# A fused attention layer on one core: another order for the first four projection units, and the first compression layer in pairs

## What is computed

```
h = rmsnorm(x, g_norm)
proj = einsum('bsd,de->bse', h, w_in)               # 2048 -> 7704 columns
... = split(proj)                                   # q, k, v, z of MoBA; q, 3 x (k, v), gates, z of NSA
y_moba = rmsnorm(o_moba * silu(m_z), g_out_moba)    # full causal attention here, since 256 tokens are one block
k_c = silu(flat(n_kc blocks + pe_ck) @ w_ck1) @ w_ck2   # 15 blocks of 32 tokens, 4096 -> 256 -> 128, per kv group
v_c = silu(flat(n_vc blocks + pe_cv) @ w_cv1) @ w_cv2
o_nsa = gates0 * compressed + gates1 * selected + gates2 * window
out = rmsnorm(x + concat(y_moba, rmsnorm(o_nsa * silu(n_z), g_out_nsa)) @ w_out, g_final)
```

## Time and profile before

| | us |
|---|---|
| time, median of 3 runs | 513.79 (513.75 to 514.21) |
| the profiled execution's own time | 515.05 |
| its span, first to last instruction | 513.2 |
| TensorE busy in the span | 502.2 (98%) |
| VectorE busy | 294.5 (57%) |
| ScalarE busy | 234.7 (46%) |
| GpSimd busy | 63.0 (12%) |
| mean granted TensorE clock | 0.997 |

### The profile page before, as it was taken

One profiled execution on the slowest core, in us unless ns is written; L12 is line 12 of the kernel. 1 busy time (PEld: TensorE's weight loads), 2 busy tenths in 40 slices (PEclk: granted clock), 3 DMA queues, 4 the chain that ended last, 5 costly groups with the idle time before them and its releaser, 6 DMA issues.

```text
span 513.2 us, 6503 instructions
## 1 busy us (share of the span) xinstructions
PE 502.2 (98%) x2600; PEld 415.8 (81%) x2600; DVE 294.5 (57%) x476; ACT 234.7 (46%) x323; POOL 63.0 (12%) x68
## 2 busy tenths in 40 slices
PE   7999999999999999999999999999999999999993
PEld 6878777777888888888888888888888888888882
DVE  3697434424475765955574675655366666645541
ACT  3585242434354453354345344545454562545421
POOL 3231000001010210100021030002131030011020
PEclk9999999999999999999999999999999999999998
DMA  8889469694526354344434435444985447275313
GB/s 284 294 256 358 165 247 318 243 331 134 197 90 191 137 164 137 112 163 140 152 119 163 128 119 175 156 162 141 370 307 167 163 165 245 83 245 205 123 44 120
DMA packets 53902, 96.45 MB, mean 188 GB/s; under 512 B 4240, under 2 KB 13040, under 8 KB 53488
## 3 DMA queue, kind: packets, MB, share of 16 engines
q1 hardware_dynamic: 50688, 95.43, 54.4%
q10 hardware_dynamic: 3184, 0.61, 0.7%
HBM read 93.93 MB, written 2.10 MB: 187 GB/s over the span
## 4 chain that ended last, share of the span: by engine, by line
PE 97%; DMA 1%; DVE 0%; ACT 0%; DVEq 0%; POOLq 0%; issue 0%; SPq 0%; POOL 0%
PE proj L433 27%; PE proj L435 27%; PE proj L434 27%; PE b_o L654 4%; PE b_t L419 2%; PE b_s L588 2%; PE b_s L531 2%; PE b_p L624 2%; PE b_t L678 1%; PE b_s L587 1%; DMA xo<-in_x_dram 1%; PE b_o L567 1%; PE b_o L419 0%; PE b_p L419 0%; PE b_s L419 0%; ACT raw_e L850 0%
## 5 line engine op out<-in xcount | busy, mean ns | idle before, releaser
L945 DVE TENSOR_TENSOR w_lo<-w_raw,w_hi 128x2048 fp32r<-128x2048 f32 x72 | 166.9, 2321 | 105.2 <-ACT w_hi L727 105.2
L433 PE MATMUL proj<-w_hi,xT_hi 128*128 128x512 f32 x536 | 216.6, 404 | 0.1
L435 PE MATMUL proj<-w_hi,xT_lo 128*128 128x512 f32 x536 | 209.3, 391 | 0.0
L434 PE MATMUL proj<-w_lo,xT_hi 128*128 128x512 f32 x536 | 208.7, 389 | 0.0
L727 ACT ACTIVATE w_hi<-w_raw 128x2048 fp32r<-128x2048 f32 x72 | 137.5, 1912 | 44.6 <-PE proj L435 35.4
L433 PEld LDWEIGHTS proj<-w_hi,xT_hi 128*128 128x128 f32 x536 | 100.7, 188 | 23.4 <-issue 3.6
L435 PEld LDWEIGHTS proj<-w_hi,xT_lo 128*128 128x128 f32 x536 | 100.6, 188 | 21.7
L434 PEld LDWEIGHTS proj<-w_lo,xT_hi 128*128 128x128 f32 x536 | 100.8, 188 | 19.9
L384 POOL TENSOR_TENSOR rope_a<-rope_a,rope_b 128x512 f32<-128x512 f32 (+1 forms) x16 | 24.2, 1534 | 237.9 <-DVE rope_b L1015 237.9
L779 ACT ACTIVATE Q<-b_t 128x512 f32<-128x512 f32 x18 | 10.8, 598 | 60.2 <-PE b_t L419 60.2
L791 ACT ACTIVATE pT<-b_p 128x384 f32<-128x384 f32 x24 | 11.7, 487 | 55.9 <-PE b_p L624 55.9
(11 more groups left out here) (187 smaller groups left out, 434.7 us busy)
## 6 DMA issues: line engine op xcount, KB each, us to landing
w_raw<-in_w_in_dram SPq DMA_DIRECT2D x57, 1024.0 KB, 5.2
w_raw<-in_w_out_dram SPq DMA_DIRECT2D x16, 1024.0 KB, 5.1
xo<-in_w_ck_dram SPq DMA_DIRECT2D x4, 1024.0 KB, 5.8
xo<-in_w_cv_dram SPq DMA_DIRECT2D x4, 1024.0 KB, 5.5
w_raw<-in_w_in_dram SPq DMA_DIRECT2D x12, 256.0 KB, 6.9
Q<-in_x_dram SPq DMA_DIRECT2D x1, 2048.0 KB, 10.9
out_dram<-Q SPq DMA_DIRECT2D x4, 512.0 KB, 3.1
xo<-in_x_dram SPq DMA_DIRECT2D x3, 512.0 KB, 8.0
```

Source lines behind the costliest of these rows:

```text
L433: nc.tensor.matmul(dst, a_hi, b_hi, start=first, stop=False)
L434: nc.tensor.matmul(dst, a_hi, b_lo, start=False, stop=False)
L435: return nc.tensor.matmul(dst, a_lo, b_hi, start=False, stop=last)
L945: nc.vector.tensor_tensor(wl, w_raw[:, u % RAW], wh.bitcast(F32), ALU.subtract).then_inc(lo_ready, 1)
```

## The change

Four things are edited.

1. The first four units on TensorE are written out in another order. A product now waits only for its own operands: hi·hi for `xT_hi` and `w_hi`, lo·hi (`LH`) for `xT_lo`, hi·lo (`HL`) for `w_lo`, which comes last in each unit. Rounds 2 and 3 come after 12 products of unit 0, rounds 4 and 5 after 8 of unit 1, rounds 6 and 7 after 8 of unit 2.
2. The start of TensorE: 6 identity products instead of 4, then the gain's transpose, then each of rounds 0 and 1 followed by one identity product and one identity transpose; the 15 identity products are gone.
3. The second half of the first quarter of x is issued by ScalarE's queue. ScalarE and VectorE do their pieces of units 0 to 3 in another order.
4. The pieces of the first compression layer are multiplied two by two, in slots 7, 10, 13 and 16, and have a load table of their own.

```diff
-NBUSY = 15
-X_ROUNDS_AT = {(0, 2): 2, (1, 2): 4, (1, 5): 6}
+ORDER_0 = [(HH, 0, 0), (HH, 0, 1), (LH, 0, 0), (LH, 0, 1), (HH, 1, 0), (HH, 1, 1), (HH, 0, 2), (LH, 0, 2), (HH, 0, 3), (LH, 0, 3),
+           (LH, 1, 0), (LH, 1, 1), (HH, 1, 2), (LH, 1, 2), (HH, 1, 3), (LH, 1, 3)] + [(HL, m, k) for k in range(UK) for m in range(MT)]
+X_ROUNDS_AT = {(0, 12): 2, (1, 8): 4, (2, 8): 6}
-CK_SLOT = [6, 7, 9, 10, 12, 13, 15, 16]
+CK_SLOT = [7, 7, 10, 10, 13, 13, 16, 16]
+CK_LOAD = [6, 7, 11, 12, 14, 15, 17, 18]
...
-                    for m in range(MT):
-                        sp.dma_start(xo[:, m, 0:CW], x[0, m * P:(m + 1) * P, 0:CW]).then_inc(x_in[4 * m], 16)
+                    sp.dma_start(xo[:, 0, 0:CW], x[0, 0:P, 0:CW]).then_inc(x_in[0], 16)
...
-                while ck_next < 8 and u >= CK_SLOT[ck_next] and u >= 6:
+                while ck_next < 8 and u >= CK_LOAD[ck_next]:
...
+                if kind == HH:
+                    if k == 0:
+                        pe.wait_ge(xhi_done, 2 * u + m + 1)
+                    if m == 0 and u < FIRST:
+                        pe.wait_ge(first_hi, u * UK + k + 1)
+                    if m == 0 and k == 0 and u == FIRST:
+                        pe.wait_ge(hi_ready, 1)
+                    return nc.tensor.matmul(dst, x_hi, w_hi_, start=u == 0 and k == 0, stop=False)
+                if kind == LH:
+                    if k == 0:
+                        pe.wait_ge((xlo_even, xlo_odd)[m], u + 1)
+                    return nc.tensor.matmul(dst, x_lo, w_hi_, start=False, stop=False)
+                if m == 0 and u < FIRST:
+                    pe.wait_ge(first_lo, u * UK + k + 1)
+                if m == 0 and k == 0 and u == FIRST:
+                    pe.wait_ge(lo_ready, 1)
+                return nc.tensor.matmul(dst, x_hi, w_lo_, start=False, stop=u == UPC - 1 and k == UK - 1)
...
             pe.wait_ge(ident_ok, 1)
-            keep_busy(4)
-            x_round_(0)
-            x_round_(1)
+            keep_busy(6)
             pe.wait_ge(grow_in, 16)
             nc.tensor.transpose(b_p[:, 0:KT], grows, ident[0:KT, 0:KT]).then_inc(crows_T, 1)
-            keep_busy(NBUSY)
+            x_round_(0)
+            keep_busy(1)
+            keep_busy_short(1)
+            x_round_(1)
+            keep_busy(1)
+            keep_busy_short(1)
...
             act.dma_start(grows, g_norm[0].rearrange("(k p) -> k p", p=P)).then_inc(grow_in, 16)
+            act.dma_start(xo[:, 1, 0:CW], x[0, P:2 * P, 0:CW]).then_inc(x_in[4], 16)
 
             x_hi(0)
-            first_hi_(0, [0])
+            first_hi_(0, [0, 1])
             x_hi(1)
-            first_hi_(0, [1, 2, 3])
+            first_hi_(0, [2, 3])
...
+                elif slot == 1:
                     x_g(6)
                     x_g(7)
-                    first_lo_(2, [1, 2, 3])
+                    lo(3)
                     x_lo(7)
```

More of the change, by code:

```diff
@@ L55 @@
 RAW, SPL = 3, 3
-NBUSY = 15
-X_ROUNDS_AT = {(0, 2): 2, (1, 2): 4, (1, 5): 6}
 FIRST = 3
+HH, LH, HL = 0, 1, 2
+ORDER_0 = [(HH, 0, 0), (HH, 0, 1), (LH, 0, 0), (LH, 0, 1), (HH, 1, 0), (HH, 1, 1), (HH, 0, 2), (LH, 0, 2), (HH, 0, 3), (LH, 0, 3),
+           (LH, 1, 0), (LH, 1, 1), (HH, 1, 2), (LH, 1, 2), (HH, 1, 3), (LH, 1, 3)] + [(HL, m, k) for k in range(UK) for m in range(MT)]
+ORDER_N = [(HH, m, k) for m in range(MT) for k in range(UK)] + [(LH, m, k) for m in range(MT) for k in range(UK)] + \
+          [(HL, m, k) for k in range(UK) for m in range(MT)]
+X_ROUNDS_AT = {(0, 12): 2, (1, 8): 4, (2, 8): 6}
 LAST = NSLOT - UPC
@@ L129, in heads_done @@
     return sum(ends_head(i) for i in range(j + 1))
-CK_SLOT = [6, 7, 9, 10, 12, 13, 15, 16]
-CK_AT = {s: c for c, s in enumerate(CK_SLOT)}
+CK_SLOT = [7, 7, 10, 10, 13, 13, 16, 16]
+CK_LOAD = [6, 7, 11, 12, 14, 15, 17, 18]
 CK_SUM_SLOT = [11, 17]
@@ L453, in bank_free, with first_product, first_unit @@
                     pe.wait_ge(dve_read, dve_reads(c - 2))
+            def first_product(u, kind, m, k):
+                dst, x_hi, x_lo, w_hi_, w_lo_ = operands(u, m, k)
+                if kind == HH:
[15 more added lines that the diff above has]
+                return nc.tensor.matmul(dst, x_hi, w_lo_, start=False, stop=u == UPC - 1 and k == UK - 1)
+            def first_unit(u):
+                for n, (kind, m, k) in enumerate(ORDER_0 if u == 0 else ORDER_N):
+                    if (u, n) in X_ROUNDS_AT:
+                        x_round_(X_ROUNDS_AT[u, n])
+                        x_round_(X_ROUNDS_AT[u, n] + 1)
+                    last = first_product(u, kind, m, k)
+                last.then_inc(unit_used, 1)
             def unit(u):
+                if u < UPC:
+                    return first_unit(u)
                 if u < NPROJ:
                     c, g = u // UPC, u % UPC
-                    if u < UPC:
-                        pe.wait_ge(xlo_even, u + 1)
-                        pe.wait_ge(xlo_odd, u + 1)
                 else:
@@ L466, in unit @@
                     bank_free(c)
[L467 to L478, removed]
+                pe.wait_ge(lo_ready, u - FIRST + 1)
+                for m in range(MT):
+                    for k in range(UK):
+                        last = three_products(*operands(u, m, k), g == 0 and k == 0, g == UPC - 1 and k == UK - 1)
                 last.then_inc(unit_used, 1)
@@ L678, in keep_busy, with keep_busy_short @@
                     nc.tensor.matmul(b_t[:, 0:P], ident[:, :], ident[:, :], start=True, stop=True)
+            def keep_busy_short(n):
+                for _ in range(n):
+                    nc.tensor.transpose(b_t[:, 0:P], ident[:, :], ident[:, :])
             pe.wait_ge(ident_ok, 1)
-            keep_busy(4)
-            x_round_(0)
-            x_round_(1)
+            keep_busy(6)
             pe.wait_ge(grow_in, 16)
             nc.tensor.transpose(b_p[:, 0:KT], grows, ident[0:KT, 0:KT]).then_inc(crows_T, 1)
-            keep_busy(NBUSY)
+            x_round_(0)
[4 more added lines that the diff above has]
+            keep_busy_short(1)
             for slot in range(LAST):
@@ L694, in _ @@
                     round_(slot)
-                if slot in CK_AT:
-                    ck_unit(CK_AT[slot])
+                for c in range(8):
+                    if CK_SLOT[c] == slot:
+                        ck_unit(c)
                 if slot in CK_SUM_SLOT:
@@ L865, in _ @@
             act.dma_start(invf[:, :], inv_freq).then_inc(trig_in, 16)
+            first_hi_(1, [0])
             x_hi(2)
+            first_hi_(1, [1])
             x_hi(3)
-            first_hi_(1, range(UK))
+            first_hi_(1, [2, 3])
             for slot in range(NSLOT):
@@ L873, in _ @@
                     first_hi_(2, range(UK))
+                elif slot + 2 < NSLOT:
+                    hi(slot + 2)
+                if slot == 1:
                     x_hi(6)
                     x_hi(7)
-                elif slot + 2 < NSLOT:
-                    hi(slot + 2)
                 if slot == 1:
@@ L1157, in _ @@
             x_lo(1)
-            first_lo_(0, [1, 2, 3])
+            first_lo_(0, [1, 2])
             x_g(2)
             x_g(3)
+            first_lo_(0, [3])
             first_lo_(1, [0])
             x_lo(3)
-            first_lo_(1, [1, 2, 3])
+            first_lo_(1, [1, 2])
             for slot in range(NSLOT):
@@ L1167, in _ @@
                     x_g(5)
+                    first_lo_(1, [3])
                     first_lo_(2, [0])
                     x_lo(5)
+                    first_lo_(2, [1, 2, 3])
+                elif slot == 1:
                     x_g(6)
                     x_g(7)
-                    first_lo_(2, [1, 2, 3])
+                    lo(3)
                     x_lo(7)
```

## The result

The changed kernel took 509.95 us (median of 4, 509.06 to 512.04), the kernel before 514.0 (513.75 to 514.66) in the same comparison: a ratio of 0.9923, 95% interval 0.9902 to 0.9944, which is 2.9 to 5.0 us less. The forecast was 507.9, in a range of 506.9 to 510.5. The profiled execution took 510.15, with a span of 508.3 where before had 513.2: 4.9 us less, against 5.9 in the forecast's sum. Of all the executions told of here one, of the kernel with products for transposes, took 631 us at a granted clock of 0.753 (all others 0.988 or more), and its ratio is taken without it.

The account below looks back on a forecast made before the run. The prediction took TensorE, busy 98% of the span, as the bound, with about 13 us before unit 0. Start 5.2 plus pairs 1.2, less 0.5 for the clock, took the median from 513.79 to 507.9 us, range 506.9 to 510.5.

Parts of the forecast that it names:

- the forecast's sum: Whole kernel: 5.2 us from the start plus 1.2 from the pairs, less 0.5 for the clock.
- The slower rival: Units 0 and 1: no fast TensorE clock until well into unit 1, eating the whole gain (514.1) or giving 520; chance 0.05.
- the prediction's own signs of being wrong: Early proj products 0.45 apart, TensorE waiting for `w_hi` or `xT_lo` in units 1 to 3, or a later stall.
- Part 1 and 2: Start and unit 0: unit 0 begins at 7.6 to 8.4 instead of 12.93, unit 1 at 14.5, 4.9 us earlier.
- my rival of the late clock: Unit 0's first 12 products at the low clock: 3.1 us lost, 510.5; half of them, 509; chance 0.22.
- The 0.5 that I allowed: Unit 0: 0.5 us taken off the gain for a clock not yet fast when the unit starts.
- Part 3: Units 1 to 3: VectorE keeps up with slack of 1.3 to 2.8, the old 0.29 wait goes; 5.2 us earlier at unit 4.
- Part 4: Compression pieces in pairs: three lone pieces save 0.32 each, slot 12 another 0.2; 1.2 us in all.
- slot 13's row: Profile row before the change: a piece directly followed by like work takes 0.92, against 1.24 for one alone.
- The step from the profiled execution to the median: Whole kernel: profiled 515.05 would become 509.2, and so the median of 513.79 becomes 507.9.
- the slack of 1.0: Unit 3: if GpSimd waits behind VectorE's `w_lo`, xT_lo(6) is ready at 28.0, wanted at 29.0.

Follow-up runs that it names:

- products for transposes: Changed kernel with the two identity transposes at the start written as identity products; ratio 0.9901 to the kernel before, from three executions.
- the changed kernel's second: The changed kernel timed and traced once more, unchanged, against the kernel before: 509.23 us, ratio 0.9898.
- start alone: Changed kernel with the old slots and loads of the compression layer, so only the reordered start: 510.88 us, ratio 0.9939 to the kernel before.
- four more: Changed kernel with 5 identity products instead of 1 between round 1 and unit 0: 509.57 us, ratio 0.9904 to the kernel before.
- loads late: Changed kernel with ScalarE's three issues of gate columns and second-layer weights moved from slot 1 to slot 6: 508.77 us, ratio 0.9891.
- both: Changed kernel with all three of ScalarE's loads in slot 6 and two more identity products ahead of unit 0: 508.75 us, ratio 0.9900.
- the run with the gate columns late: Changed kernel with only the gate columns' load moved to slot 6, second-layer weight loads staying in slot 1: 508.38 us, ratio 0.9888.

## Why the prediction was right or wrong

**Direction and mechanism: right.** Unit 0 no longer stands behind identity products and all its operands; rounds 2 and 3 did not wait for x, units 1 to 3 did not wait for `w_hi`, `xT_lo` or `w_lo`, and the pairs saved time. The slower rival did not come, and at most 0.1 was lost after slot 16. But two of the prediction's own signs of being wrong came in the first trace: early products 0.43 apart, and TensorE idle at unit 4, which began at 34.22 instead of 32.6. The range went up to 510.5 for the first of them. The second, 0.54 us, was in no term, and that the pairs gave 0.4 more than forecast beside it is luck.

**Size: forecast 5.9 to 6.1, measured 4.0 and 5.1.** In the two first traces the sum can be checked to the tenth. It had 6.36 without the clock; the spans differ by 4.9:

- *Part 1 and 2, unit 1 at 14.5.* It was 15.74 in the first trace, 1.24 later: 0.5 from unit 0's start (8.10, inside my 7.6 to 8.4) and 0.8 from its first twelve products (3.99 us instead of 3.2) at the low level. Only the 0.8 is my rival of the late clock, which I had priced at 1.6 us for half of the products (509 against 507.4) and 3.1 for all; seven of the twelve ran slowly here. The 0.5 is not the clock at unit 0: five of the six traces with an early clock begin unit 0 at 8.00 to 8.11 as well. It sums from round 0 (4.85, not 4.6), x_g(0) (6.08, not 5.75) and the first `w_hi` block. In the six traces with an early clock (the changed kernel's second, start alone, four more, products for transposes, loads late, both) unit 1 begins at 14.6 to 14.9, 0.1 to 0.4 after the 14.5 of Part 2. The 0.5 that I allowed is too much for those, and too little for the two late ones (15.74, and 15.78 in the run with the gate columns late).
- *Part 3, slack of units 3 to 5.* VectorE was in time for unit 3, but not by my account. Its `w_lo` began 1.4 late (25.79, not 24.4) and yet ended at 28.07 against 28.0, since GpSimd did not lengthen it as I had counted; x_lo(7) then waited for GpSimd and ended at 29.79 against 28.6, ahead of its use at 31.2. The step that failed is the unstated one, that ScalarE would be ready for unit 4's `w_hi` when VectorE was. I had counted ScalarE's activations and not its issues in slot 1. In the trace of before the issue took 1.3 us and lay under unit 3's `w_hi` (27.04 to 28.94); now it stands behind x_hi(7), takes 2.97, and lies on the way to unit 4. Cost 0.54, shown by the loads moved away. Why the same issue took 1.2 to 1.4 us in the four traces with the old order and 2.9 to 3.0 in those with the new stays open.
- *Part 4, the pairs.* 1.2 forecast, 1.6 in the traces. The second piece costs 0.86 (2.10 less 1.24), not the 0.92 of slot 13's row, and each of four visits saved about 0.4.
- *1.24 + 0.54 + 0.08 in units 1 and 2, less 0.4 for the pairs, is 1.46*, the difference of 6.36 and 4.90.

**The step from the profiled execution to the median failed.** I subtracted 5.9 from 515.05 and took the same 5.9 off 513.79. But the profiled execution of before was 1.3 above that median, and at least part of it sat in the very stretch that the change replaces: thirty records of identity products that take 5.86, 5.64 or 5.02 us by when the clock rises, so that unit 0 began at 12.93 in that trace and at 11.96 in another of the same start. What the change saves is then up to 1.0 less in an ordinary execution than in the profiled one. With unit 0 at 12.3 for before (between the traces) and at 8.0 after, the start gives 4.3 less 0.4 in unit 0 and 0.5 for the issue plus 0.29 for the wait of before, 3.7, where 3.1 (2.5 to 3.8) was measured. How far that holds for medians is argued from three traces of before, not shown for all executions. The median of three, 513.79, was itself low: over the 26 executions of before that stand beside the first experiments it is 514.38, and the profiled execution's surplus is then 0.7, not 1.3.

**VectorE and GpSimd.** The timeline of the changed kernel at unit 3's `w_lo`:

```profile
25.79 2.28 DVE L982 TENSOR_TENSOR w_lo<-w_raw,w_hi 128x2048 fp32r<-128x2048 f32 x1
26.02 3.22 POOL L363 TENSOR_TENSOR xT_lo<-rope_b,xT_hi 128x512 fp32r<-128x512 f32 x1 [4.75 <-ACT xT_hi L770]
27.99 1.80 DVE L1004 TENSOR_TENSOR xT_lo<-rope_b,xT_hi 128x512 fp32r<-128x512 f32 x1
```

GpSimd, which comes second, takes 3.22 instead of 1.29 and ends 1.2 after VectorE's `w_lo`; then VectorE's next, 1.80 instead of 0.68, ends 0.55 after GpSimd. That agrees with the Trainium skill ("SBUF — State Buffer", "SBUF: two separate sides"), that the two exclude each other for a whole instruction, whichever is first. xT_lo(6) was ready at 29.24 and wanted at 30.31; the slack of 1.0 worked out ahead was there.

## What to carry to other kernels

Ask of each product which of its operands is late, and put the products with late operands last: here the early start gave nothing with the old order of products, and taking out identity products without the new order gave 0.7. Where the profiled execution is above its median, look whether the surplus lies in what the change removes before the difference is carried over. Count an engine's issues among its work when its order moves, above all one that follows a load like the gate columns' here.

## What was not expected of the hardware

- The moment at which TensorE's spacing halves (a round of four transposes from 1.12 to 0.60 or 0.65 us, a product from 0.43 to 0.227) moved between about 4.9 and 10.8 us in eight traces whose work up to there was alike, and unit 1's start with it by 1.1 us. The granted clock, 1.00 there, does not show it. That the moment differs between executions agrees with the Trainium skill, "TensorE: Matmul & The Clock Gate", Part 1. That page gives half a microsecond either way for it, and here it moved by almost 6.
- An issue of a 128 KB load took 0.38 us, but 1.3, 2.97, 4.66 and 5.03 in four of the traces in which it stood directly behind a load of 2048 pieces of 128 bytes on the same queue. The issue of that load itself took 0.38 each time: the price is paid by the next one.
- After a wait of 2.85 us TensorE was back at the lower level, where waits of about 1 us (the changed kernel's second trace) left it at the higher.
